# Last projection of a two-block transformer in two token halves, on weights held in the gather ring

## The reference, cut to what matters

```python
mixed = sigmoid(g_s) * y_s + sigmoid(g_m) * y_m          # (256, 1024)
h = h + mixed @ w_out[l]                                 # the last projection
h = h + peer_ffn(rmsnorm_2(h, norm2_g[l]), peer_w_q[l], peer_sub_keys[l], peer_u[l], peer_v[l])
return rmsnorm_2(h, final_norm_g)[:, N_META:]
```

## Time and profile before

| what | value |
|---|---|
| median of three runs (lowest, highest) | 1936.19 us (1935.8, 1937.76) |
| profiled execution, its own time | 1936.39 us |
| span of its profile | 1934.6 us |
| PE, DVE, ACT, POOL busy in the span | 1804.0, 1145.7, 949.7, 1224.1 us |
| moved by DMA | 486.76 MB, of which 268.45 MB by the gathers' queue |

### The profile page before, as it was taken

How to read it: one execution, slowest core, us unless ns; L and a number is a source line. 1 busy time by engine, 2 the same in 40 slices (tenths; PEclk the granted TensorE clock), 3 DMA queues, 4 the chain that set the end, 5 groups by cost and what they waited for, 6 DMA issues and landing times.

```text
span 1934.6 us, 29255 instructions
## 1 busy us (share of the span) xinstructions
PE 1804.0 (93%) x9861; PEld 1366.0 (71%) x9864; DVE 1145.7 (59%) x2481; ACT 949.7 (49%) x1757; POOL 1224.1 (63%) x708
## 2 busy tenths in 40 slices
PE   8999999999999999999999999999999877778777
PEld 7999888999999998789998878875544322222222
DVE  5444555444644466754457775576677666777664
ACT  5444646444544465654448445454444444444443
POOL 8888665888788877388887962534444343433441
PEclk9999999999999999999999999999999999999999
DMA  7666443666566555266654341599999999999996
GB/s 269 186 186 190 152 144 125 197 189 185 169 196 188 185 167 166 80 188 188 187 184 140 122 152 55 154 389 421 421 421 421 421 421 418 421 422 419 422 420 283
DMA packets 98426, 486.76 MB, mean 252 GB/s; under 512 B 11920, under 2 KB 12944, under 8 KB 65312
## 3 DMA queue, kind: packets, MB, share of 16 engines
q1 hardware_dynamic: 60304, 213.20, 35.6%
q0 software_dynamic: 36864, 268.45, 33.4%
q10 hardware_dynamic: 1168, 3.96, 0.6%
HBM read 484.10 MB, written 1.05 MB: 251 GB/s over the span
## 4 chain that ended last, share of the span: by engine, by line
PE 68%; DMA 16%; DVE 5%; ACT 5%; POOL 4%; issue 2%; DVEq 0%; ACTq 0%; POOLq 0%
DMA arena<-uv_tab,arena 16%; PE ps L827 16%; PE ps L2608 10%; PE ps L178 8%; PE ps L179 8%; PE ps L180 8%; PE ps L825 7%; PE ps L208 2%; POOL split L1824 2%; PE ps L2553 2%; DVE arena L2794 1%; ACT arena L2482 1%; PE ps L209 1%; PE ps L830 1%; POOL arena L1828 1%
## 5 line engine op out<-in xcount | busy, mean ns | idle before, releaser
L553 POOL TENSOR_TENSOR split<-raw,split 128x1024 fp32r<-128x1024 f32 x358 | 859.0, 2407 | 292.6 <-ACT split L228 287.9
L228 ACT ACTIVATE split<-raw 128x1024 fp32r<-128x1024 f32 x382 | 404.7, 1063 | 494.7 <-PE ps L180 263.0
L2608 PE MATMUL ps<-arena 128*128 128x512 f32 x1024 | 494.2, 617 | 101.7 <-ACT arena L2482 101.4
L2659 POOL DMA_INDIRECT arena<-uv_tab,arena x256 | 268.4, 1049 | 383.8 <-PE ps L2608 350.9
L827 PE MATMUL ps<-xs,split 128*128 128x512 f32 x1344 | 470.6, 393 | 0.0
L2608 PEld LDWEIGHTS ps<-arena 128*128 128x128 f32 x1024 | 181.9, 191 | 400.6 <-ACT arena L2482 248.2
L825 PE MATMUL ps<-xs,split 128*128 128x256 f32 x1176 | 328.5, 279 | 0.0
L827 PEld LDWEIGHTS ps<-xs,split 128*128 128x128 f32 x1344 | 247.0, 188 | 43.5
L825 PEld LDWEIGHTS ps<-xs,split 128*128 128x128 f32 x1176 | 221.1, 188 | 6.9
L2794 DVE CUSTOM_DVE_ANT_0 arena<-arena,raw 128x1024 f32<-128x1024 f32 x128 | 156.8, 1225 | 103.9 <-DMA arena<-uv_tab,arena 103.2
L2794 DVE CUSTOM_DVE_ANT_0 arena<-arena 128x1024 f32<-128x1024 f32 x128 | 156.9, 1226 | 91.4 <-DMA arena<-uv_tab,arena 90.6
(11 more groups left out here) (424 smaller groups left out, 2742.2 us busy)
## 6 DMA issues: line engine op xcount, KB each, us to landing
raw<-wstream SPq DMA_DIRECT2D x393, 512.0 KB, 3.5
over_split<-wstream SPq DMA_DIRECT2D x8, 512.0 KB, 6.6
arena<-uv_tab,arena POOLq DMA_INDIRECT x256, 15.1
arena<-small SPq DMA_DIRECT2D x1, 1195.0 KB
arena<-xT SPq DMA_DIRECT2D x1, 1024.0 KB, 6.2
arena<-keys ACTq DMA_DIRECT2D x1, 1024.0 KB, 7.9
arena<-rows ACTq DMA_DIRECT2D x1, 512.0 KB, 4.5
over_h<-wstream SPq DMA_DIRECT2D x1, 512.0 KB, 8.4
```

The source lines that it names most:

```text
L228: act.activation(parts_of(k, m)[0], raw_slot(k, m), ACT.Copy).then_inc(k.hi_done, 1)
L553: pool.tensor_tensor(lo, raw_slot(k, n), hi.bitcast(F32), ALU.subtract).then_inc(k.lo_done, 1)
L2608: last = pe.matmul(ps[:, banks[t][0] + i, :], diag[:, n % 4, :], ring[n % NS][:, D + i * 512:D + (i + 1) * 512], start=False, stop=ends, s ...
L2659: pool.indirect_dma_start(ring[n % NS], None, ins["uv_tab"], bass.IndirectOffsetOnAxis(ap=ids[:, b, s:s + 1], axis=0)).then_inc(k.px_in[n ...
```

## The change

The last projection is taken out of `add_projection` and moved into `peer`. Its weights are no longer split into parts: SP loads the 8 packets as they are into `w_last`, which is the memory of four of the eight ring buffers, as soon as the mLSTM branch is done, and the query packets behind them. DVE writes the mixed chunks to SBUF in full precision, and nothing splits them. PE computes the projection in plain fp32 in two token halves (`last_part(n, t)`): 8 tiles for the first 128 tokens, query tiles 0 and 1 for these tokens, tile 0 of the second half, the scores of head 0, the sum of squares, then tiles 1 to 7 of the second half, and only behind them `turn` and query tiles 2 and 3. Query tiles 0 to 3 are now all done in token halves, and those for the second 128 tokens stand ahead of slot 0. The second tokens' sum of squares moves into slots 14 to 20 (`PE_NORM_AT`). The ring is turned so that gathers 4 to 7 go to the `w_last` memory; each waits until two more of the projection's tiles are complete.

```diff
--- before.py
+++ after.py
+PE_NORM_AT = 18
...
+        w0, p0 = AT["w_out"], AT["peer_q"]
+        full = w0 // RAW
+        assert w0 % RAW == 0
...
-        for n in range(full * RAW, last):
-            sp.wait_ge(k.lo_done, n - RAW + 1)
-            sp.dma_start(k.raw[:, n % RAW, :], wstream[n]).then_inc(k.landed[n % RAW], 16)
+        sp.wait_ge(k.mix_ready, 3 * DC)
+        for j in range(DC):
+            sp.dma_start(k.w_last[:, j, :], wstream[w0 + j]).then_inc(k.last_in[j // 2], 16)
+        sp.dma_start(query_slot(k, 14), wstream[p0 + 14]).then_inc(k.query_in[4], 16)
+        for n in range(RAW):
+            sp.wait_ge(k.lo_done, w0 + n - RAW + 1)
+            sp.dma_start(query_slot(k, n), wstream[p0 + n]).then_inc(k.landed[n % RAW], 16)
         for j in range(2 * SPLIT):
 
             if j % 2 == 0:
-                sp.wait_ge(k.tile_done, p0 - SPLIT + j // 2 + 1)
-            sp.dma_start(query_slot(k, RAW + j), wstream[last + j]).then_inc(k.query_in[j], 16)
-        sp.dma_start(query_slot(k, 14), wstream[p0 + 14]).then_inc(k.query_in[8], 16)
-        sp.wait_ge(k.tile_done, p0 + 1)
-        sp.dma_start(query_slot(k, 15), wstream[p0 + 15]).then_inc(k.query_in[9], 16)
+                sp.wait_ge(k.tile_done, w0 - SPLIT + j // 2 + 1)
+            sp.dma_start(query_slot(k, RAW + j), wstream[p0 + RAW + j]).then_inc(k.query_in[j // 2], 16)
+        sp.dma_start(query_slot(k, 15), wstream[p0 + 15]).then_inc(k.query_in[5], 16)
...
+        def total(n, lo=0, hi=SEQ):
+            b, s = ps[:, bank[n], lo:hi], k.sig[:, 8 + n, lo:hi]
+            k.dve(dve.tensor_tensor(b, b, k.sig[:, 16 + n, lo:hi], ALU.mult))
+            k.dve.settle(dve)
+            dve.tensor_tensor(s, b, s, ALU.add).then_inc(k.mix_ready, 1)
+
+        dve.wait_ge(k.sig_made, 3)
+        for n in range(DC):
             dve.wait_ge(k.tile_done, packet + n + 1)
-            b = ps[:, bank[n], 0:SEQ]
-            k.dve(dve.tensor_tensor(b, b, k.sig[:, 16 + n, :], ALU.mult))
-            k.dve.settle(dve)
-            dve.tensor_tensor(b, b, k.sig[:, 8 + n, :], ALU.add).then_inc(k.mix_sum, 1)
-
-        def rest(c):
-            dve.wait_ge(k.mix_high, c + 1)
-            dve.tensor_tensor(k.xs[:, 1, c, 0:SEQ], ps[:, bank[c], 0:SEQ], k.xs[:, 0, c, 0:SEQ].bitcast(F32), ALU.subtract
-                              ).then_inc(k.mix_ready, 1)
-
-        dve.wait_ge(k.sig_made, 3)
-        for n in range(7):
-            total(n)
-        for c in range(late):
-            rest(c)
-        total(7)
-        for c in range(late, DC):
-            rest(c)
-
-    add_projection(k, block, AT["w_out"], k.mix_ready, k.mixes, tuple(range(DC)), GAIN["norm2"], by_chunk=True, first=5, whole=True)
+            if n < DC - 1:
+                total(n)
+            else:
+                total(n, 0, P)
+                total(n, P, SEQ)
+    ring = ring[4:] + ring[:4]
...
+    ring.insert(2, k.small_all[:, old:old + 2 * D])
+    ring.insert(3, k.sq.rearrange("p c t -> p (c t)")[:, 0:2 * D])
...
-        square(0)
+        for c in range(DC):
+            scaled(0, c)
+            if c in (2, 4, 6):
+                square(0, c // 2 - 1)
         half(0, 0)
-        square(1)
-        square(2)
         half(1, 0)
-        half_scores(0)
-        square(3)
+        half_scores(0, 0)
+        square(0, 3)
         act.preload_act_table(ACT.Sqrt)
+        columns(0)
+        half(2, 0)
+        half(3, 0)
+        half_scores(1, 0)
+        act.wait_ge(k.pr_rcol, 1)
+        exponentials(0)
+        for c in range(DC):
+            scaled(1, c)
         half(0, 1)
         half(1, 1)
-        columns_act(k, act, cq)
-        half_scores(1)
-        act.wait_ge(k.pr_rcol, 1)
-        exponentials(0)
-        for n in range(2, PE_TILES_FIRST):
-            tile(n)
-            if n % 2:
-                scores(n // 2)
+        half_scores(0, 1)
+        half(2, 1)
+        half(3, 1)
+        half_scores(1, 1)
         for n in range(SLOTS):
+            if PE_NORM_AT - 4 <= n < PE_NORM_AT:
+                square(1, n - PE_NORM_AT + 4)
+            if n == PE_NORM_AT + 2:
+                columns(1)
...
+        def last_part(n, t, lo=0, hi=DC):
+
+            if t == 0 and lo == 0:
+                pe.wait_ge(k.last_in[n // 2], 32)
+                if n >= 2:
+                    pe.wait_ge(k.dve_emptied, emptied + n - 1)
+            if t and n % 4 == 0:
+                pe.wait_ge(k.dve_emptied, emptied + DC - 1 + n // 4)
             for c in range(lo, hi):
-                if n == t == 0:
-                    pe.wait_ge(k.xl_ready, DC * e0 + c + 1)
-                last = pe.matmul(ps[:, n + 2 * t, t * P:(t + 1) * P], w[:, c, :], k.over_xs[:, 0, c, t * P:(t + 1) * P],
+                if n < 2 and t == 0:
+                    pe.wait_ge(k.mix_ready, sums + max(c, 5) + 1)
+                if n == 0 and t == 1 and c == DC - 1:
+                    pe.wait_ge(k.mix_ready, sums + DC + 1)
+                last = pe.matmul(area(n, t), k.w_last[:, n, c * P:(c + 1) * P], mixed[:, c, T[t]],
                                  start=(c == 0), stop=(c == DC - 1))
             if hi == DC:
-                last.then_inc(k.tile_done if t else k.pr_half, 1)
-
-        def half_scores(t):
+                last.then_inc(k.tile_done if t else k.last_half, 1)
...
+        last_part(0, 0, 0, DC - 1)
+        last_part(1, 0, 0, DC - 1)
+        last_part(0, 0, DC - 1, DC)
+        last_part(1, 0, DC - 1, DC)
+        for n in range(2, DC):
+            last_part(n, 0)
         half(0, 0)
         half(1, 0)
-        half(0, 1, 0, 2)
-        pe.wait_ge(k.pr_q, 2)
+        last_part(0, 1)
         pe.wait_ge(k.keys_in, 16)
-        half_scores(0)
-        half(0, 1, 2, DC)
-        half(1, 1)
-        pe.wait_ge(k.sq_sum, r + 1)
-        columns_pe(k, pe, cq)
-        tiles.wait_emptied(pe, 1)
-        pe.wait_ge(k.pr_sc, 1)
-        half_scores(1)
+        half_scores(0, 0)
+        columns(0)
+        for n in range(1, DC):
+            last_part(n, 1)
+        turn(0, 6)
+        half(2, 0)
+        half(3, 0)
         pe.wait_ge(k.col_rms, cq + 1)
-        turn(0, 6)
-        for n in range(2, PE_TILES_FIRST):
-            tile(n)
-            if n % 2:
-                scores(n // 2)
+        half_scores(1, 0)
         pe.wait_ge(k.pr_ht, 1)
         begin(0)
+        half(0, 1)
+        half(1, 1)
+        half_scores(0, 1)
+        half(2, 1)
+        half(3, 1)
+        half_scores(1, 1)
         for n in range(SLOTS):
+            if n == PE_NORM_AT + 1:
+                pe.wait_ge(k.pr_sc, 6)
+                columns(1)
...
-            if n == NS - 1:
-                pool.wait_ge(k.col_rms, cq + 1)
-                pool.wait_ge(k.pr_sqdone, 1)
+            if NS // 2 <= n < NS:
+                pool.wait_ge(k.tile_done, w0 + 2 * (n - NS // 2) + 2)
...
+        def added(n, t):
+
+            dve.wait_ge(*((k.tile_done, w0 + (n | 3) + 1) if t else (k.last_half, n + 1)))
+            dve.tensor_tensor(x[:, n, T[t]], area(n, t), x[:, n, T[t]], ALU.add).then_inc(k.dve_emptied, 1)
+
+        def squares(t, first, last):
+            for i in range(first, last):
+                dve.wait_ge(k.sq_ready, 4 * (r + t) + i + 1)
+                step = dve.tensor_tensor(sq[:, 0:2, :], sq[:, 0:2, :], sq[:, 2 * i:2 * i + 2, :], ALU.add)
+                if i < 3:
+                    k.dve(step)
+                    k.dve.settle(dve)
+                else:
+                    step.then_inc(k.sq_sum, 1)
+
+        for n in range(DC):
+            added(n, 0)
+        squares(0, 1, 3)
...
+        for n in range(DC):
+            added(n, 1)
         for g in range(GROUPS):
             steps = list(route(g + 1)) if g + 1 < GROUPS else []
             for s in range(PE_K):
                 dot(g * PE_K + s)
+                if g * PE_K + s == PE_NORM_AT:
+                    squares(1, 1, 4)
+                if g * PE_K + s == PE_NORM_AT + 2:
+                    inverse(1)
```

156 lines of the change are left out of this document (87 added, 69 removed).

## The result

The changed kernel takes **1952.65 us** (median of 4, 1949.15 to 1953.69) against 1936.32 us (1935.8 to 1937.76): a ratio of 1.008, 95% interval 1.0065 to 1.0095. It is slower by 16.3 us. Its profiled execution spans 1951.0 us against 1934.6, 16.4 more.

What follows compares the result with a forecast made beforehand. The prediction took the never-pausing stream of 256 gathers as the bound, its end moved by the first scores and slot 0. Gather 8's 9.8 us plus 1.4 made 11.2, on 1936.39: 1947.6 us; own range 1945 to 1951, wide 1939.5 to 1953.

Steps and rivals of the forecast that it cites:

- the wide range: End time from 1939.5, every PE wait hidden, to 1953, norm taking 2.2 us and PE losing 2 to 3 more.
- First clock: The first scores, which start the gather stream, come 5.8 us earlier; gather 0 issued at 1266.9.
- PE's work: Matmuls from the last projection to slot 0: 51 us, with 1.87 us for an fp32 tile half.
- The waits: PE idle ahead of slot 0: 8 us in all, including 2.6 before the square sum and 1.1 for second tokens' x.
- The restart: Stream stands still 17.6 us after gather 7; gather 8 lands 9.8 us later than before, gather 10 adds 1.4.
- the waits pull PE's clock down: Rival: ahead of slot 0 PE's clock falls twice, stretching fp32 matmuls to double; 3 us more, 1950.6; chance 0.08.
- Norm in the slots: Second tokens' norm, slots 14 to 20: PE stands 3 to 4 us, costing 0; rival 2.2 us, 1949.8, chance 0.07.
- The weights: SP's loads from about 1226 us, done near 1261, before the gathers; cost taken as nothing.
- Early start: Rival: the stream never runs dry and all gathers land 7.8 us earlier, 1928.6; chance 0.08.
- overlap: Rival: DVE and ACT feed PE sooner, slot 0 near 1294 to 1295; some 3 us lost, 1939.5; chance 0.07.
- my bound for hidden waits: With every PE wait hidden, slot 0 starts at 1293.9 and the end comes 3.1 us later: 1939.5.

Runs made afterwards that it cites:

- experiment 1: Changed kernel with gather 0 also waiting for all 16 tile halves of the last projection: 1952.33 us.
- experiment 6: Changed kernel with the second tokens' query halves moved to slots 88 to 95, and gather 0 held back until the fourth second-half part: 1933.11 us.
- experiment 3: Changed kernel with 12 zero bf16 matmuls, whose results nobody uses, in PE's wait just ahead of slot 0: 1948.97 us.
- experiment 4: Changed kernel with the first sum of squares behind two second-half parts: 1946.4 us; with 12 zero matmuls ahead of slot 0 and ACT's exponential earlier too: 1943.56 us.

## Why the prediction was right, and what was mis-sized

The direction and the mechanism held: the start of the stream came earlier, slot 0 later, the stream stood still once, and the end followed slot 0. The size did not: 16.3 us slower where I gave 9 to 14, and 1952.65 us lies above the forecast's own range, 1945 to 1951. It is inside the wide range, 1939.5 to 1953, by 0.35 us, and that is in part luck: I had put the upper end there for a norm that takes 2.2 us and 2 to 3 us lost by PE, and the norm took nothing. Two other things filled the room, the clock and the restart.

**First clock.** Right: gather 0 at 1266.53 (1266.9 predicted), gather 7 landing at 1292.1 (1290.4). And right that the start does not set the end: 15 us later in experiment 1 and 4.2 us later in experiment 6, it cost nothing.

**PE's work.** Right. A part is 1.80 us from its start to that of the next (the last six of the first half 10.80 us, the seven of the second half 12.59 us in experiment 3), against the 1.87 that I took; the row's 10.96 us has the tail of its last matmul in it. The start of the work was 0.4 us later than in the earlier trace rows, and by the first scores the shorter parts had made that good (1263.37; predicted 1263.7).

**The waits.** Right to 0.1 us: 2.66 (2.6), 1.07 (1.1), 2.81 (2.8). They were read from the order of ACT's and DVE's steps and their durations in the earlier trace rows. Slot 0 came at 1303.22 instead of 1302.0: the seven parts took 14.2 instead of 13.1 us, because of the first fall of the clock, and the rest is within 0.2 us. The terms of my own list, added up again, give 1301.8 and not 1302.0: those behind the first chunk at 1289.5 are 9.5 us, which ends at 1299.0 and not at 1299.2.

**The restart: the mis-sized term.** I gave slot 0 at 1302.0, 2.8 us from there to gather 8's issue, 5.7 for its landing and 1.4 more until gather 10, with all later gathers as late as that: +11.2. Measured +16.4. The 5.2 us between are, step by step along the gathers:

- slot 0 itself, 1.2;
- slot 0 to the issue of gather 8, 4.56 instead of 2.76 us, 1.8: slot 0 ran at half clock. Experiment 3 takes it away (2.77 us);
- gather 8's landing, 5.9 instead of 5.7, 0.2;
- gathers 8 to 10, issues 7.46 us apart instead of 6.4, and a landing 0.5 shorter than gather 8's: 0.5, so that gather 10 is 3.7 us later than predicted;
- gather 10 to 11, landings 4.0 us apart instead of 2.49, 1.5. With 69 fillers in the kernel before it is 4.2, at full clock: this part belongs to the restart, not to the clock.

Of the 5.2 us some 3.4 are thus the clock (1.1 ahead of slot 0, 1.8 and 0.5 behind it; gather 255 of experiment 3 is 3.4 us earlier) and 1.5 the ramp. The rival that gave this, that the waits pull PE's clock down, had 3 us as its price and 1950.6 us as its time; its mechanism is real and its size was right. It had a chance of 0.08 because the row that spoke for it showed one short fall with PE half busy; I should have asked for each of the three waits that I had just worked out whether such a fall goes with it. The ramp was in no rival, though the kernel before shows steps like it where its stream starts: gather 1 lands at 1281.6 us and gather 2, issued 1.24 us behind it, at 1284.8, 3.2 us later.

The Trainium skill (TensorE: Matmul & The Clock Gate, Part 1) has the throttled clock as the default that activity releases; the trace agrees, with 0.51 behind the wait of 2.81 us and 1.00 where fillers stand in it. By the Trainium skill (DMA: Bandwidth & Descriptors, "Anatomy of one DMA — SWDGE (gpsimd) path") a gather in an empty queue would land after 4.4 us, an estimate from its formula; in six restarts here it was 5.2 to 7.0 us, 5.7 in the mean, so the rows' 5.7 was the better price.

**Norm in the slots.** Right at 0: PE waits 0.86 and 1.53 us at slots 20 to 22 (I had 3 to 4), and the window from 1350 to 1360 us still has a DMA share of 1.01 and 420 GB/s. The difference is 16.5 us at gather 11 and again at gather 64.

**The weights.** Right: SP issues them between 1226.8 and 1249.6 us, the median of the slowest group lands after 15.2, and no row of PE waits for one.

**Early start, overlap.** Both rivals fell: the kernel with all three moves of experiment 4 still loses 7.2 us, where my bound for hidden waits had 3.1. Slot 0 is at 33.5 us there, not at the 30.9 of the bound (1293.9 in the table's count), since PE still stands, or runs fillers, for ACT's table load and copies, and the ramp adds its 1.5: 3.1 + 2.6 + 1.5 = 7.2.
